# Block inputs taken between the steps of plain tiles, and their rounding one tile earlier

## The reference

```python
def swiglu(x, w_gu, w_down):
    gate, up = jnp.split(x @ w_gu, 2, axis=-1)
    return (jax.nn.silu(gate) * up) @ w_down

# in trunk, for each layer l
x = x + 0.5 * rmsnorm(swiglu(rmsnorm(x, n[0]), w1_gu[l], w1_down[l]), n[1])
m, S_a, S_r = mixer(rmsnorm(x, n[2]), pos, w_in[l], ...)
x = x + rmsnorm(m, n[3])
x = x + 0.5 * rmsnorm(swiglu(rmsnorm(x, n[4]), w2_gu[l], w2_down[l]), n[5])
```

## Time and profile before

| | |
|---|---|
| time, median of 3 runs | 2149.12 us (2148.87 to 2149.69) |
| the profiled execution | 2149.47 us, span 2147.7 us |
| TensorE busy | 2108.6 us (98%) |
| VectorE busy | 1302.9 us (61%) |
| ScalarE busy | 941.8 us (44%) |
| GpSimd busy | 860.1 us (40%) |
| TensorE's granted clock, mean | 0.998 of full speed |

### The profile page before, as it was taken

How to read it: one execution, slowest core, us unless ns; L and a number is a source line. 1 busy time by engine, 2 the same in 40 slices (tenths; PEclk the granted TensorE clock), 3 DMA queues, 4 the chain that set the end, 5 groups by cost and what they waited for, 6 DMA issues and landing times.

```text
span 2147.7 us, 43008 instructions
## 1 busy us (share of the span) xinstructions
PE 2108.6 (98%) x17095; PEld 2080.3 (97%) x17095; DVE 1302.9 (61%) x1995; ACT 941.8 (44%) x1727; POOL 860.1 (40%) x708
## 2 busy tenths in 40 slices
PE   8999999999999999999999999999999999999998
PEld 8999999999989999999999999999999899999998
DVE  5988700587367888840189885007863788888202
ACT  5445433442344554543354454334424454544333
POOL 3433344443315433344544334453432345333442
PEclk9999999999999999999999999999999999999999
DMA  5234442322234233442423345332222343344422
GB/s 152 81 110 127 148 140 85 92 79 72 67 97 138 70 89 116 131 158 85 118 61 89 110 126 169 115 109 66 80 69 60 97 138 89 89 120 123 157 87 75
DMA packets 389341, 224.54 MB, mean 105 GB/s; under 512 B 9780, under 2 KB 380264, under 8 KB 387880
## 3 DMA queue, kind: packets, MB, share of 16 engines
q1 hardware_dynamic: 372208, 213.19, 33.9%
q10 hardware_dynamic: 16952, 8.81, 1.4%
HBM read 200.41 MB, written 21.56 MB: 103 GB/s over the span
## 4 chain that ended last, share of the span: by engine, by line
PE 88%; DVE 7%; issue 3%; ACT 2%; POOL 1%; DMA 0%; DVEq 0%; SPq 0%; POOLq 0%; ACTq 0%
PE ps L715 54%; PE ps L772 28%; PE ps L947 1%; DVE x L1994 1%; DVE xb L1797 1%; DVE y L1988 1%; POOL w_lo L636 1%; DVE xs_lo L1748 1%; DVE w_lo L1852 0%; PE ps L1109 0%; PE ps L1126 0%; PE ps L1021 0%; DMA x_tok<-in_x_prompt_dram 0%; ACT o_hi L1627 0%; PE ps L1048 0%
## 5 line engine op out<-in xcount | busy, mean ns | idle before, releaser
L636 POOL TENSOR_TENSOR w_lo<-raw,w_hi 128x384 fp32r<-128x384 f32 (+1 forms) x452 | 558.1, 1244 | 677.3 <-ACT w_hi L1315 677.2
L1315 ACT ACTIVATE w_hi<-raw 128x384 fp32r<-128x384 f32 (+1 forms) x452 | 246.9, 559 | 455.9 <-PE ps L715 451.8
L772 PE MATMUL ps<-xb,w_hi 128*128 128x272 f32 x2048 | 388.3, 288 | 4.7 <-DVE w_lo L1852 4.4
L715 PE MATMUL ps<-xs_hi,w_hi 128*128 128x288 f32 (+1 forms) x1568 | 345.2, 292 | 5.0 <-DVE xs_lo L1748 4.2
L715 PE MATMUL ps<-xs_hi,w_lo 128*128 128x288 f32 (+1 forms) x1568 | 340.1, 288 | 0.0
L715 PE MATMUL ps<-xs_lo,w_hi 128*128 128x288 f32 (+1 forms) x1568 | 339.5, 288 | 0.0
L772 PEld LDWEIGHTS ps<-xb,w_hi 128*128 128x128 f32 x2048 | 321.4, 188 | 7.1 <-DVE w_lo L1852 3.7
L772 PE MATMUL ps<-xb,w_lo 128*128 128x272 f32 x1024 | 295.3, 288 | 0.0
L715 PEld LDWEIGHTS ps<-xs_hi,w_hi 128*128 128x128 f32 x1568 | 257.2, 188 | 12.2 <-DVE xs_lo L1748 6.2
L715 PE MATMUL ps<-h_hi,w_lo 128*128 128x256 f32 x1272 | 267.2, 289 | 0.0
L715 PE MATMUL ps<-h_lo,w_hi 128*128 128x256 f32 x1272 | 266.1, 288 | 0.0
(11 more groups left out here) (264 smaller groups left out, 3761.8 us busy)
## 6 DMA issues: line engine op xcount, KB each, us to landing
raw<-in_w_gu_dram SPq DMA_DIRECT2D x176, 512.0 KB, 4.2
raw<-in_w_in_dram SPq DMA_DIRECT2D x56, 512.0 KB, 3.8
raw<-in_w_down_dram SPq DMA_DIRECT2D x64, 384.0 KB, 3.4
raw<-in_w_down_dram SPq DMA_DIRECT2D x64, 320.0 KB, 3.1
h_away<-low_away SPq DMA_DIRECT2D x44, 272.0 KB, 4.5
h_lo<-h_away SPq DMA_DIRECT2D x8, 1088.0 KB, 7.5
raw<-in_w_out_dram SPq DMA_DIRECT2D x16, 512.0 KB, 3.9
ret_state<-in_state_ret_dram SPq DMA_DIRECT2D x8, 512.0 KB, 6.6
```

What stands on the lines that cost most here:

```text
L636: pool.tensor_tensor(lo, raw[:, u, k0:k0 + n, :], hi.bitcast(F32), ALU.subtract)\
L715: mm = pe.matmul(bank_part(bank, a), w, v[:, k, TOK[a]], start=(start and n == 0), stop=(stop and n == 2))
L772: mm = pe.matmul(ps[:, j, 0:TH], w[j][:, k, :], xb[:, c_, part, k, :], start=(k == 0 and m == 0), stop=(k == KH - 1 and m == 2))
L1315: act.activation(hi, raw[:, u, k0:k0 + n, :], ACT.Copy).then_inc(hi_split, 1)
```

## The change

On VectorE the table is gone and the order is written out. The eight block inputs are taken one at a time between the scale, product and low steps of plain tiles 0 and 1, with the last four behind tile 1's low step. The low parts of inputs 4 and 5 stand between the steps of tile 2, the low part of input 6 and the third sum between those of tile 3. On ScalarE the three roundings move one plain tile earlier: inputs 4 and 5 behind tile 1, input 6 behind tile 2, in each case ahead of that tile's weight halves. No instruction is added or removed, and the orders on TensorE, GpSimd and SP are unchanged.

```diff
                 for t in range(TILE0 - 1):
                     plain_tile(l, f, t)
                     plain_high(l, f, t)
-                    if t == 2:
+                    if t == 1:
                         xb_split(l, f, 4)
                         xb_split(l, f, 5)
-                    elif t == 3:
+                    elif t == 2:
                         xb_split(l, f, 6)
                     if t < TILE0 - 2:
                         for u in ((1,) if t == 0 else (2 * (t % 2), 2 * (t % 2) + 1)):
...
-            def norm_inputs(l, f):
-
-                for k in range(KD):
+            def norm_inputs(l, f, *ks):
+
+                for k in ks:
...
-                behind = {1: lambda: norm_inputs(l, f),
-                          2: lambda: (xb_low(l, f, 0), xb_low(l, f, 1), input_sum(l, f, 1), input_sum(l, f, 2)),
-                          3: lambda: (xb_low(l, f, 2), input_sum(l, f, 3), input_sum(l, f, 4))}
-                for t in range(TILE0 - 1):
-                    plain_scale(l, f, t)
-                    plain_product(l, f, t)
-                    plain_low(l, f, t)
-                    if t in behind:
-                        behind[t]()
+                plain_scale(l, f, 0)
+                norm_inputs(l, f, 0)
+                plain_product(l, f, 0)
+                norm_inputs(l, f, 1)
+                plain_low(l, f, 0)
+                plain_scale(l, f, 1)
+                norm_inputs(l, f, 2)
+                plain_product(l, f, 1)
+                norm_inputs(l, f, 3)
+                plain_low(l, f, 1)
+                norm_inputs(l, f, 4, 5, 6, 7)
+                plain_scale(l, f, 2)
+                xb_low(l, f, 0)
+                plain_product(l, f, 2)
+                xb_low(l, f, 1)
+                plain_low(l, f, 2)
+                input_sum(l, f, 1)
+                input_sum(l, f, 2)
+                plain_scale(l, f, 3)
+                xb_low(l, f, 2)
+                plain_product(l, f, 3)
+                input_sum(l, f, 3)
+                plain_low(l, f, 3)
+                input_sum(l, f, 4)
+                plain_scale(l, f, 4)
+                plain_product(l, f, 4)
+                plain_low(l, f, 4)
```

## The result

| | before | after |
|---|---|---|
| time, median of 6 runs | 2149.40 us | 2157.49 us (2156.95 to 2157.83) |
| ratio | | 1.0037, 95% interval 1.0026 to 1.0048 |
| span of the profiled execution | 2147.7 us | 2155.2 us |

Here the kernel before was timed again beside the changed one. The changed kernel is 8.1 us slower. Predicted were 2157.5 us and a loss of 8.4, counted from the earlier median of 2149.12.

The account below looks back on a forecast made before the run. TensorE, busy 98% of the span, was taken as the bound. Stalls of 1.36 and 0.84 us cost three feedforwards 2.20 each and the first 1.80: +8.4 on 2149.12 gives 2157.5 us, 8-in-10 range 2153.3 to 2162.6.

Parts of the forecast that it names:

- VectorE's pieces: Block inputs in plain tiles 0 and 1: third piece held up by GpSimd, last four 0.70 us each with GpSimd idle.
- First stall: Plain tile 3, each up stage: TensorE waits for weights queued behind ScalarE's rounding that needs the last block input; 1.36 us.
- Second stall: Plain tile 4, each up stage: weights queued behind block 6's rounding, which waits for VectorE's second input sum; 0.84 us.
- Nothing given back: Pair windows: VectorE starts from TensorE's end of tile 5 as before, so none of the lost time is regained.
- The rival that ends faster: Work done earlier carries into the first pair windows, removing TensorE's 6.8 us and 0.24 there: 2142.1 us; chance 0.05.
- The first feedforward: Loses 1.80 us and not 2.20 like the other three, because it already had a wait of 0.40.
- Sum: All four feedforwards: three lose 2.20 us each and one 1.80, in all +8.4 us, giving 2157.5 us, +0.39%.
- The clock: TensorE's pauses of 1.2 and 0.7 us bring no clock fall; rival: one fall per up stage, +15.6, 2164.7 us, chance 0.08.

Follow-up runs that it names:

- the roundings alone: Kernel before with only ScalarE's three roundings moved as in the change, VectorE's order as before: 2169.85 us, ratio 1.0095.
- inputs 4 and 5 behind the weights: Changed kernel with ScalarE's roundings of inputs 4 and 5 behind tile 3's weight halves, input 6's still ahead of tile 4's: 2148.96 us, ratio 0.9997.
- the roundings between the weights: Changed kernel with ScalarE's rounding of input 5 between tile 3's two weight tiles and input 6's between those of tile 4: 2148.6 us, ratio 0.9997.
- the pieces alone: Changed kernel with only VectorE's block inputs piece by piece in tiles 0 and 1; tiles 2 and 3 and the roundings as before: 2148.6 us.

## Why the prediction was right

- **VectorE's pieces.** Forecast: the third is held up by GpSimd, ends where the product ended before and moves the product by 0.7; the last four are 0.70 apart. Measured: 1.70 us for the third, 2.87 for the last four, which is 0.70 apart and 0.77 for the last. With GpSimd at work the same four take 5.86. That the four run undisturbed because the delay itself leaves GpSimd without work was the step that decided between 1.4 and 5.5 us.
- **First stall.** Forecast 1.36, measured 734.20 + 0.69 = 734.89 to 736.27: 1.38. Its cause is shown by the roundings alone (3.5 when the last block input is later), and by the kernels in which it goes when only ScalarE's order changes (inputs 4 and 5 behind the weights, and the roundings between the weights).
- **Second stall.** Forecast 0.84, measured 12.75 − 12.05 = 0.70. The chain was the forecast one, operation by operation, and came out 0.14 us shorter over some eight handovers between VectorE and GpSimd: 745.88 for the rounding where 745.33 + 0.69 = 746.02 was forecast. The steps behind it fit operations that wait GpSimd's out whole, as the prediction played them.
- **Nothing given back.** True in three feedforwards: VectorE's idle time before tile 5's scaling grew from 0.54 to 1.70, and the waits in the pair windows stayed. The rival that ends faster falls by the same row that spoke against it. In the fourth it is not true. The prediction worked out the second feedforward and took the others to have the same spacings, but the longest wait of 1.0 us in the earlier trace rows stands in the fourth alone, and 0.35 us of it was given back.
- **The first feedforward** lost 1.70 us, forecast 1.80, because it had some 0.4 us of this loss already.
- **Sum.** 1.70 + 2.07 + 2.08 + 1.71 = 7.56, forecast 8.4. Measured are 8.1 between the medians and 7.5 between the spans. The mechanism was right; that the median came out at 2157.49, on the very number, is luck, since the traced loss is 0.8 us below the forecast and the kernel before was 0.3 us slower this time.
- **The clock.** It stayed up at pauses of 1.2 and 0.5 us, as forecast. Whether it falls after 3.3 us was not decided by the length of the pause alone.

## What to carry to other kernels

On an engine with a fixed order, look at what stands behind a waiting instruction, not only at what it waits for: here two roundings of 1 us each, at 733 and 746 us, of inputs that TensorE does not multiply before the pair windows, from 773 us on, held back the weights of the next tile. An operation whose input is not ready goes behind the work that feeds the bounding engine, even where that work has some microseconds to spare: the wait can be longer than they are. And filling the idle time of an engine that later waits for the bound anyway moves the idle time and gains nothing: the pieces alone gave a ratio of 0.9995, within the noise.

## What was not expected of the hardware

With pauses of TensorE of 3.32 to 3.36 us, in one execution, the granted clock fell in two of four places (the second and fourth feedforward) and stayed at 1.00 in the others. A pause of 2.45 us outside the up stages had been enough in the kernel before. In the second feedforward it fell at about 740.1, 2.0 us after TensorE stopped, and stayed low until about 747.0, so it cost some 2.5 us and not the 1.8 that the earlier case gives. What decides between the two was not tried.
